# A 31-tap depthwise convolution moves from ScalarE and GpSimd to TensorE, and the steps around it stand in another order

## The reference, cut to what matters

```
def _conformer_conv(v, gt, w_dw, b_dw, ln_g, ln_b, w_pw):
    u = v * jax.nn.sigmoid(gt)
    u = _causal_depthwise_conv(u, w_dw, b_dw)          # 31 taps, 256 channels
    u = jax.nn.silu(_layernorm(u, ln_g, ln_b))
    return u @ w_pw
...
    y_a = _pool_mixer(p_pool, pool_w[l], pool_scale[l])
    y_b = _conformer_conv(p_bval, p_bgate, ...)
    y_c = _rglru_branch(p_cgate, p_cx, ...)            # 4-tap convolution, two gates, scan
    y = jnp.concatenate([y_a, y_b, y_c], axis=-1)
    h = h + y @ w_out[l]
```

## Time and profile before

| | us |
|---|---|
| three runs, median (lowest, highest) | 1353.49 (1351.45, 1354.27) |
| the profiled execution | 1353.51 |
| its span | 1351.7 |
| TensorE busy | 1257.9 (93%) |
| VectorE busy | 875.0 (65%) |
| ScalarE busy | 618.9 (46%) |
| GpSimd busy | 118.4 (9%) |

### The profile page before, as it was taken

One profiled execution on the slowest core, in us unless ns is written; L12 is line 12 of the kernel. 1 busy time (PEld: TensorE's weight loads), 2 busy tenths in 40 slices (PEclk: granted clock), 3 DMA queues, 4 the chain that ended last, 5 costly groups with the idle time before them and its releaser, 6 DMA issues.

```text
span 1351.7 us, 17623 instructions
## 1 busy us (share of the span) xinstructions
PE 1257.9 (93%) x6213; PEld 1026.2 (76%) x6213; DVE 875.0 (65%) x1165; ACT 618.9 (46%) x940; POOL 118.4 (9%) x88
## 2 busy tenths in 40 slices
PE   7899999999988999999998799777999999999997
PEld 5687778777866887777776589775888888888885
DVE  5978888888963456666667667997655522455322
ACT  6456556655652244655565555654332212222112
POOL 0011110111100000000000003581000000000000
PEclk9999999999999999999999799888999999999998
DMA  5333233323323332222221132211323333333332
GB/s 153 110 94 110 78 94 108 94 78 95 107 63 101 93 94 78 74 68 62 65 75 47 40 93 71 63 48 40 97 85 98 99 95 93 93 93 93 109 93 78
DMA packets 203289, 115.57 MB, mean 85 GB/s; under 512 B 3456, under 2 KB 201216, under 8 KB 202224
## 3 DMA queue, kind: packets, MB, share of 16 engines
q1 hardware_dynamic: 201472, 104.50, 26.7%
q0 software_dynamic: 1776, 10.53, 2.3%
HBM read 112.85 MB, written 2.16 MB: 85 GB/s over the span
## 4 chain that ended last, share of the span: by engine, by line
PE 62%; DVE 25%; issue 6%; ACT 6%; DMA 1%; DVEq 0%; SPq 0%; ACTq 0%; POOL 0%
PE psum L510 57%; DVE w_lo L1366 5%; ACT w_hi L922 2%; DVE arena L1801 2%; DVE arena L1439 2%; DVE arena L1657 2%; DVE arena L1440 1%; PE psum L695 1%; DVE arena L1504 1%; DVE mixw L1528 1%; DMA w_raw<-a_w_in 1%; DVE mixw L1532 1%; ACT arena L1119 1%; ACT L1119 1%; DVE arena L1441 1%
## 5 line engine op out<-in xcount | busy, mean ns | idle before, releaser
L922 ACT ACTIVATE w_hi<-w_raw 128x1024 fp32r<-128x1024 f32 x191 | 202.1, 1058 | 503.8 <-PE psum L510 502.0
L510 PE MATMUL psum<-a_hi,w_hi 128*128 128x512 f32 (+1 forms) x1000 | 362.0, 381 | 14.1 <-DVE w_lo L1366 14.1
L510 PE MATMUL psum<-a_lo,w_hi 128*128 128x512 f32 (+1 forms) x1000 | 356.9, 376 | 0.0
L1366 DVE TENSOR_TENSOR w_lo<-w_raw,w_hi 128x1024 fp32r<-128x1024 f32 x191 | 257.4, 1348 | 150.6 <-ACT w_hi L922 150.4
L510 PE MATMUL psum<-a_hi,w_lo 128*128 128x512 f32 (+1 forms) x1000 | 354.7, 373 | 0.0
L510 PE MATMUL psum<-b_hi,w_hi 128*128 128x512 f32 x640 | 256.2, 400 | 8.3 <-DVE b_lo L1545 4.1
L510 PE MATMUL psum<-b_lo,w_hi 128*128 128x512 f32 x640 | 255.2, 399 | 0.0
L510 PE MATMUL psum<-b_hi,w_lo 128*128 128x512 f32 x640 | 253.8, 397 | 0.0
L510 PEld LDWEIGHTS psum<-a_hi,w_hi 128*128 128x128 f32 x1000 | 184.2, 192 | 52.8 <-issue 16.7
L510 PEld LDWEIGHTS psum<-a_hi,w_lo 128*128 128x128 f32 x1000 | 184.3, 192 | 34.0
L510 PEld LDWEIGHTS psum<-a_lo,w_hi 128*128 128x128 f32 x1000 | 184.0, 192 | 31.9
(11 more groups left out here) (269 smaller groups left out, 1317.9 us busy)
## 6 DMA issues: line engine op xcount, KB each, us to landing
w_raw<-a_w_in SPq DMA_DIRECT2D x49, 512.0 KB, 3.9
w_raw<-w_up SPq DMA_DIRECT2D x32, 512.0 KB, 4.0
w_raw<-w_down SPq DMA_DIRECT2D x32, 512.0 KB, 3.7
arena<-acs POOLq DMA_DIRECT2D x8, 1024.0 KB, 5.1
w_raw<-a_w_out SPq DMA_DIRECT2D x16, 512.0 KB, 3.8
w_raw<-w_kv SPq DMA_DIRECT2D x16, 512.0 KB, 3.9
w_raw<-b_w_in SPq DMA_DIRECT2D x16, 512.0 KB, 3.9
w_raw<-w_in SPq DMA_DIRECT2D x14, 512.0 KB, 3.7
```

Source lines behind the costliest of these rows:

```text
L510: ins = mm(out, wv[:, u.par, k, :], xv[:, k0 + k, c0:c0 + cn], start=(first and begin and i == 0 and n == 0), stop=(last and end and i == ...
L922: ac(w_hi[:, u.par, :, :], w_raw[:, u.par, :, :], ACT.Copy).then_inc(S["hi_ready"], 1)
L1366: tt(w_lo[:, u.par, :, :], w_raw[:, u.par, :, :], f32(w_hi[:, u.par, :, :]), ALU.subtract).then_inc(S["lo_ready"], 1)
```

## The change

The second channel tile of the 31-tap convolution is no longer made by ScalarE and GpSimd. The host passes in 31 diagonal matrices with the tap weights (`dwdiag`, padded to 32), eight to a unit, and four more units c0 to c3 stand between the projection's steps. They pass through the same load, high and low halves; TensorE multiplies each diagonal matrix with the tile shifted by the tap, split in high and low parts (`cu_hi`, `cu_lo`), into one bank: 24 products of 512 columns for c0 to c2, 21 for c3. ScalarE then adds the bias in one instruction.

The order is now that of `IN2_STEPS`. The gate sets stand behind steps 5, 6, 8 and 9, in two long and two short pieces with banks of their own. The four projections of the gate branch (steps 10 to 13) leave out the 16 meta tokens and are one product of 512 columns each (`in2_gate`). The first transposes stand behind step 10, the second in front of step 13. On VectorE the layer norm's work moves to step 11, the scans of tiles 2 and 3 stay at step 12 and at the end, the pool means move to steps 10 and 12, and the first tile's taps are spread otherwise. Each step's elementwise work still stands behind that step's high half on ScalarE, and behind its eviction and low half on VectorE. GpSimd waits for the two split copies before the pooling.

```diff
-U_OUT2 = U_IN2 + 14
+U_OUT2 = U_IN2 + 18
+IN2_STEPS = (0, 1, 2, 3, 4, "c0", 5, "c1", 6, "c2", 7, "c3", 8, 9, 10, 11, 12, 13)
...
-            for n, c in enumerate(IN2_TILES):
-                load(Lin(U_IN2 + n), t["w_in_2"], 0, Lin(c * P))
+            for i, n in enumerate(IN2_STEPS):
+                if isinstance(n, str):
+                    load(Lin(U_IN2 + i), t["dwdiag"], KT * int(n[1]), Lin(0))
+                else:
+                    load(Lin(U_IN2 + i), t["w_in_2"], 0, Lin(IN2_TILES[n] * P))
...
-            for k in range(1, DW_K):
-                pool.wait_ge(S["prod_ready"], k + 1)
-                if k > 1:
-                    pool.wait_ge(S["prod_used"], k - 1)
-                nc.gpsimd.tensor_tensor(dwo[:, 1, :], dwo[:, 1, :], products[k % 4][:, 0:SEQ], ALU.add
-                                        ).then_inc(S["prod_used"], 1)
...
+            def in2_gate(n):
+
+                u, m = Lin(U_IN2 + IN2_STEPS.index(n)), Lin(M_IN2 + n)
+                pe.wait_ge(S["acc_read"], (m - 1).v)
+                pe.wait_ge(S["lo_ready"], (u + 1).v)
+                for k in range(KT):
+                    for i, (wv, xv) in enumerate(((w_hi, a_hi), (w_hi, a_lo), (w_lo, a_hi))):
+                        ins = mm(bank(2 * m.par), wv[:, u.par, k, :], xv[:, k, META:T2],
+                                 start=(k == 0 and i == 0), stop=(k == KT - 1 and i == 2), skip_group_check=True)
+                ins.then_inc(S["unit_done"], 1)
+
+            def tap_tile(c):
+
+                u = Lin(U_IN2 + IN2_STEPS.index(f"c{c}"))
+                if c == 0:
+                    pe.wait_ge(S["rr_ready"], 3)
+                    pe.wait_ge(S["cuh_ready"], 1)
+                    pe.wait_ge(S["cul_ready"], 1)
+                pe.wait_ge(S["lo_ready"], (u + 1).v)
+                for j in range(KT):
+                    k = KT * c + j
+                    if k == DW_K:
+                        break
+                    at = DW_K - 1 - k + META
+                    for i, (wv, xv) in enumerate(((w_hi, cu_hi), (w_hi, cu_lo), (w_lo, cu_hi))):
+                        ins = mm(bank(4), wv[:, u.par, j, :], xv[:, at:at + SEQ], start=(k == 0 and i == 0),
+                                 stop=(k == DW_K - 1 and i == 2), skip_group_check=True)
+                ins.then_inc(S["unit_done"], 1)
...
+            in2(4)
+            tap_tile(0)
+            in2(5)
+            gates(0)
+            tap_tile(1)
+            in2(6)
+            gates(1)
+            tap_tile(2)
+            in2(7)
+            tap_tile(3)
+            in2(8)
+            gates(2)
+            in2(9)
+            gates(3)
+            in2_gate(10)
+
+            pe.wait_ge(S["dw_ready"], 1)
+            pe.wait_ge(S["cvo_ready"], 1)
+            pe.wait_ge(S["acc_read"], M_IN2 + 10)
...
+            in2_gate(11)
+            in2_gate(12)
 
             pe.wait_ge(S["ln_ready"], 1)
+            pe.wait_ge(S["rga_ready"], 4)
...
+            in2_gate(13)
...
+                if n == 3:
+                    act.wait_ge(S["cu_ready"], 1)
+                    ac(cu_hi[:, META:], cu[:, 1, META:], ACT.Copy).then_inc(S["cuh_ready"], 1)
+                if n == "c1":
+                    gate_sigmoids(0)
+                if n == "c2":
+                    gate_sigmoids(1)
+                    gate_exps((0, 1))
+                if n == "c3":
+                    gate_roots((0, 1))
                 if n == 8:
-                    gate_roots((0, 1))
...
+                    act.wait_ge(S["unit_done"], U_IN2 + 12)
+                    ac(dwo[:, 1, :], bank(4), ACT.Identity, bias=par[:, C_DWB + 1:C_DWB + 2]).then_inc(S["cvo_ready"], 1)
+                if n == 9:
+                    gate_sigmoids(2)
                 if n == 10:
+                    gate_sigmoids(3)
                     gate_exps((2, 3))
                 if n == 11:
-                    gate_roots((2, 3))
-                if n == 12:
                     act.wait_ge(S["ln_stat"], 1)
                     root(stat_at(N_SD), bnag[:, :, 1], eps2, 1.0, S["ln_sd"])
+                    gate_roots((2, 3))
...
-            TAPS = {1: 3, 2: 5, 3: 3, 4: 2, 5: 2, 6: 1, 7: 1, 8: 3, 9: 5, 10: 5, 11: 1}
+            TAPS = {1: 2, 2: 5, 3: 2, 4: 2, "c0": 4, 5: 2, "c1": 4, 6: 2, "c2": 4, 7: 2, "c3": 2}
...
+                if n == 10:
+                    means(0)
                 if n == 11:
+                    layer_norm_sums()
                     one_minus_a2(2)
                     one_minus_a2(3)
+                    layer_norm()
                 if n == 12:
-                    layer_norm_sums()
                     scan(2)
-                    layer_norm()
-            means(0)
-            means(1)
+                    means(1)
             lo(Lin(U_OUT2 + 1))
             scan(3)
```

More of the change, by code:

```diff
@@ L460, in _ @@
             pool.wait_ge(S["xc_ready"], 4)
+            pool.wait_ge(S["cuh_ready"], 1)
+            pool.wait_ge(S["cul_ready"], 1)
             for j in range(2):
@@ L813, in gates @@
                     pe.wait_ge(S["rga_ready"], j)
[L814 to L818, removed]
+                mm(bank(5), bdw[:, 2 + j, :], xc[:, j, 0:512], start=True, stop=True, skip_group_check=True)
+                mm(bank(6)[:, 0:16], bdw[:, 2 + j, :], xc[:, j, 512:T2], start=True, stop=True, skip_group_check=True)
@@ L820, in _ @@
+                mm(bank(6)[:, 16:512], bdw[:, 6 + j, :], xc[:, j, 0:496], start=True, stop=True, skip_group_check=True)
+                mm(bank(7)[:, 0:32], bdw[:, 6 + j, :], xc[:, j, 496:T2], start=True, stop=True, skip_group_check=True
+                   ).then_inc(S["rg_ready"], 1)
             pe.wait_ge(S["bd_in"], 16)
             pe.wait_ge(S["pw_in"], 16)
[L822 to L834, removed]
-                if n == 12:
[L837 to L844, removed]
@@ new lines, in _ @@
+            in2(1, ks=range(5))
+            pe.wait_ge(S["nrs_ready"], 2)
+            spread(bank(5), stat_at(N_RS), TOKENS1, S["nrb_ready"])
+            tp(bank(7)[:, 0:META], stat[0:META, N_R2 + 4:N_R2 + 5].to_broadcast([META, P]), ident[0:META, 0:META])
+            spread(bank(4), stat_at(N_R2), TOKENS1, S["nrb_ready"])
+            in2(1, ks=range(5, KT))
+            in2(2)
+            in2(3)
+            in2(4)
[3 more added lines that the diff above has]
+            tap_tile(1)
@@ new lines, in _ @@
+            in2(6)
[11 more added lines that the diff above has]
+            pe.wait_ge(S["acc_read"], M_IN2 + 10)
+            for i, (c0, cn) in enumerate(TOKENS1):
+                for j in range(2):
+                    ins = tp(bank(1 + 2 * (i // 2))[:, 256 * (i % 2) + P * j:256 * (i % 2) + P * j + P],
+                             dwo[:, j, c0:c0 + cn], ident)
@@ L1260, in rnn_high @@
                     ac(b_hi[:, 4 + j, 0:SEQ], xc[:, j, META:T2], ACT.Copy).then_inc(S["yh_ready"], 1)
-            PRODUCTS = {3: (0, 5), 4: (5, 9), 5: (9, 13), 6: (13, 17), 7: (17, 20), 8: (20, 24), 9: (24, 28),
-                        10: (28, 31)}
-            for n in range(14):
-                if n:
-                    hi(Lin(U_IN2 + n + 2))
+            for i, n in enumerate(IN2_STEPS):
+                if i:
+                    hi(Lin(U_IN2 + i + 2))
                 if n in (1, 3):
@@ L1857, in layer_norm_sums @@
                 for i in range(NT):
-                    own(nc.vector.bn_stats(bnst[:, i, :], psum[:, 4 + i // 2, 256 * (i % 2):256 * (i % 2) + 256]))
+                    own(nc.vector.bn_stats(bnst[:, i, :], bank(1 + 2 * (i // 2))[:, 256 * (i % 2):256 * (i % 2) + 256]))
                 own.wait()
@@ L2085 @@
         par[:, C_RGW + 4 * j:C_RGW + 4 * j + 4] = x["rg_conv_w_2"][0][:, P * j:P * j + P].T
+    diag = np.zeros((32, P, P), np.float32)
+    for k in range(DW_K):
+        diag[k] = np.diag(x["convb_dw_w_2"][0][DW_K - 1 - k, P:2 * P])
     bd = np.zeros((P, 10, P), np.float32)
```

81 lines of the change are left out of this document (35 added, 46 removed).

## The result

The changed kernel takes 1357.33 us (median of 18 runs, 1353.09 to 1360.47) against 1351.74 us for the kernel before (median of 18, 1348.99 to 1354.63). The ratio is 1.0036, with a 95% interval of 1.0028 to 1.0045: slower by 0.36%, some 5 us. The forecast was 1355.6 with a range of 1349.5 to 1360. The profiled execution took 1357.52 us with a span of 1355.7, against 1353.51 and 1351.7 before: between these two executions the difference is 4.0 us.

The account below looks back on a forecast made before the run. VectorE, slowed by GpSimd's additions, was taken to pace the stage; TensorE's added products, two waits with half clock and a shorter tail summed to 2.1 us over 1353.51: 1355.6 us, range 1349.5 to 1360.

Parts of the forecast that it names:

- VectorE's gain: Second block's input projection: without GpSimd's additions VectorE runs undisturbed, taps 0.78 us; a pair of steps costs 10.8 us.
- Rival 5: Taps slow for another reason than GpSimd, VectorE still pacing the stage: 1374 us; rivals 3 to 5 together 0.07.
- TensorE's added work: Input projection: 31 taps of three products, 21.6 us in all, a unit 5.56 us; gate set taken at 1.94.
- rival 4: Odd columns halve the tap products' rate, adding 21.6 us: 1377 us; rivals 3 to 5 together 0.07.
- First wait: TensorE before the fourth gate set, for the third set's sigmoids: 4.05 us, plus 2.8 us for half clock.
- Rival 1: Clock survives one or both waits, or waits are shorter: 1353 to 1351.3 us, 1350 with cheaper gate sets; chance 0.28.
- Table switches: ScalarE's waiting chains: each switch costed as a 1.28 us load without drain; drains would add 2.8 us.
- rival 3: Every ScalarE table switch costs a drain, adding 2.8 us: 1358.4 us; rivals 3 to 5 together 0.07.
- Second wait: TensorE before the second transposes, for a 15.5 us chain after step 10: 3.6 us, plus 1.55 for half clock.
- The tail: From step 13's end to the output projection: 10.3 us, with 0.3 for GpSimd's multiplication beside the scan, bound 1.8.
- rival 2: GpSimd's multiplication slows the last scan by 1.8 us, first waits' half clock at upper bound: 1357 to 1359; chance 0.18.
- The sum: Output projection starts at 937.5, 2.1 us later than before; everything behind it unchanged: 1355.6 us.

Follow-up runs that it names:

- e5: Kernel before with GpSimd's thirty additions cut to one column each, waits kept, part of the computation left out: 1332.1 us, ratio 0.9860.
- e1: Changed kernel with the fourth gate set behind step 10 instead of in front of it: 1347.61 us, ratio 0.9968.
- e4: Changed kernel with four unread products put into the first wait, to keep the clock: 1354.07 us, ratio 1.0010.
- e11: Changed kernel with GpSimd's third multiplication cut to one column, part of the computation left out: 1354.55 us in one execution.
- e12: The kernel before, unchanged, run once more for a second trace: 1352.13 us in one execution.
- e2: Changed kernel with the layer norm's statistics, root and scalings done earlier, on VectorE and ScalarE: 1355.86 us, ratio 1.0021.
- e3: Changed kernel with both the fourth gate set behind step 10 and the earlier layer norm: 1346.24 us, ratio 0.9958.
- e6: Changed kernel with one tap's products instead of eight in each tap unit, part of the computation left out: 1348.4 us, ratio 0.9979.
- e7: On top of e3, VectorE's second pool means moved behind the last scan: 1350.68 us, ratio 0.9985.
- e8: On top of e4, three more unread products in front of the second transposes: 1352.9 us, ratio 1.0008.
- e9: On top of e3, ScalarE's last two square roots moved behind the next high half: 1348.3 us, ratio 0.9977.
- e10: Changed kernel with the third set's sigmoids ahead of that step's high half on ScalarE: 1356.4 us, ratio 1.0041.

## Why the prediction was right, point by point

**VectorE's gain.** Right. Taps took 0.78 us start to start (3.11 us for four at 841.12 on VectorE's timeline), GpSimd was idle in this stretch until 885, and without its additions the kernel before is 20 us faster (e5). Rival 5 is out.

**TensorE's added work.** Right. A tap unit took 838.55 - 832.96 = 5.59 us where 5.56 was said; odd columns cost nothing, and rival 4 is out. A gate set took 2.06 us start to start where I took 1.94, over the upper bound of 2.0 that I gave. The old form had taken less than I read, since 1.94 is a printed duration; start to start it was 1.59 us, as two rows of the kernel before show:

```profile
876.06 1.94 PE L816 MATMUL psum<-arena,mixw 128*128 128x264 f32 x8
877.65 0.60 PE L510 MATMUL psum<-a_hi,w_hi 128*128 128x264 f32 x2
```

So the new form, two long and two short pieces, costs 0.47 us more for each set with the same columns, and twice that at half clock (4.20 against 3.28). Step 9 ended near 890.3 and not at 889.5: 0.36 from three gate sets, 0.28 from a start that was later in this execution, 0.1 from the tap units.

**First wait.** 3.90 us where 4.05 was said, released by the sigmoids; the 3.90 counts from the modelled end of the last product, and from 890.3, as the forecast counts, it is 4.1. The clock fell as assumed. The set took 4.20 us for 3.28, since I had put the old form's row in its place, and step 10 took 904.74 - 898.58 = 6.16 for 6.99, since less of the half clock was left for it; together 10.4 for 10.3. Moving one line takes wait and clock away together (e1), and unread products take the clock's part alone (e4). Rival 1 is out for this trace.

**Table switches.** From the start of the high half at 890.57 to the load are 1.07 us, to the first sigmoid at 892.94 another 1.30, to the end of the second 1.30, and 0.14 to the gate set at 894.38. The load of 1.28 us follows right on the high half and the sigmoid right on the load, with no room for a drain of 1.38. Here the Trainium skill (ScalarE: Activation LUTs, What ACT_TABLE_LOAD costs) has its load, 1283 ns, borne out and its drain not; rival 3 is out.

**Second wait.** 3.17 for 3.6, on a chain of 920.07 - 904.74 = 15.3 us for 15.5. The transposes took 1.97 us at half clock and step 13 6.33; I had charged the same loss at the other place, 0.82 and 7.1: 8.3 for 7.9. Step 13 ended at 928.4, for 927.2.

**The tail.** 10.9 us for 10.3. This is the term that was mis-sized: I charged 0.3 us for GpSimd's multiplication beside the last scan, with a bound of 1.8. Its first instruction took 1.77 for 0.70, 1.07 more (e11 takes it away). Low half and scan took 934.40 - 929.53 = 4.9 us for 3.8. This is the mechanism of rival 2, at somewhat over half of its bound, and by the 0.7 us of e11 just over the 0.6 us at which the prediction let that rival decide. Its other half, a half clock at its upper bound behind the first waits, did not come.

**The sum.** The output projection started at 939.31, not 937.5: 0.28 from the start, 0.66 before step 10's end, 0.26 by the second wait's chain and clock together, 0.61 in the tail. So the 2.1 us more that were forecast for the stage measured 3.65 in the traces: every mechanism was in place, and the gate sets, the clock behind the second wait and the overlap in the tail were each a little too small in the sum. Behind it nothing changed: it takes 1355.7 - 939.3 = 416.4 us to the end of the span, and 1351.7 - 935.4 = 416.3 before.

**The number.** 1357.33 lies 1.7 us above the forecast of 1355.6, just outside the likeliest case's own range (1353.8 to 1357.2) and inside the wide one (1349.5 to 1360). That it came so near is in part luck. The forecast added 2.1 us to 1353.51, an execution that turned out 1.8 us above the median of the kernel before; the difference itself measured 5.6 us by the medians. The two errors have opposite signs.

**What stays open.** The medians lie 5.6 us apart, the stretches 3.65, and the two profiled executions 4.0. The kernel before has the same stretch in two traces (e12), so the missing 2 us are not the waits of that kernel. Its profiled execution was 1.8 us above its median, the changed kernel's 0.2 above its own: execution against execution almost nothing is missing, and the 2 us appear only between medians of 18. The median less the stretch of the one trace gives what the rest of a kernel takes; all these kernels compute the same, or nearly so, ahead of the stretch and behind it:

| kernel | median us | stretch us | rest us |
|---|---|---|---|
| before | 1351.74 | 102.70 | 1249.0 |
| changed | 1357.33 | 106.35 | 1251.0 |
| e1 gates later | 1347.61 | 98.44 | 1249.2 |
| e2 norm earlier | 1355.86 | 105.50 | 1250.4 |
| e3 both | 1346.24 | 97.70 | 1248.5 |
| e4 keep clock | 1354.07 | 104.96 | 1249.1 |
| e5 no additions | 1332.10 | 83.88 | 1248.2 |
| e6 few products | 1348.40 | 99.46 | 1248.9 |
| e7 scan first | 1350.68 | 100.29 | 1250.4 |
| e8 keep twice | 1352.90 | 102.80 | 1250.1 |
| e9 roots later | 1348.30 | 96.71 | 1251.6 |
| e10 sigmoids first | 1356.40 | 105.80 | 1250.6 |

The rest scatters from 1248.2 to 1251.6, and in the traces the stretch starts between 828.4 and 833.0 us, though the work ahead of it is the same or nearly so. The highest, e9's, holds 1.6 us of half clock behind the stretch. The changed kernel's extra 2 us are of the size of the scatter; what decides it ahead of the stage was not looked into, and whether it is chance or belongs to a kernel's layout is open. It also means that one trace's span is no measure of a change of 0.2%; the stretch between two events is a better one, if its end takes in the clock that the last wait leaves behind.

## What to carry to other kernels

When work is moved to the engine that will then be always busy, walk that engine's queue forward and ask of each wait what the releasing engine has ahead of it. A wait for a chain that only starts when the last unit ends was paid in full here, whatever the sums of busy time said. Put one independent unit between: one line moved turned 0.36% of loss into 0.32% of gain. And price a stall on TensorE with the half clock that may follow it, here 3.9 us of wait and 2.6 of clock. Whether it follows can't be read from the wait's length alone. In the kernel before the granted clock read 0.53 behind a wait of 1.90 us and 1.00 behind one of 2.77:

```profile
848.30:851.70 3.40, 3.40 (x16) 3.40 (x17) 3.33 (x3) 1.99 (x3) 3.11 (x3) 0.53 0.53 154
...
860.40:863.90 3.50, 3.49 (x28) 3.50 (x29) 3.43 (x3) 3.40 (x5) 3.21 (x3) 1.00 0.54 151
```

## What the runs showed of the hardware that was not expected

Products that nobody reads, put into a wait, kept the granted clock up: with 0.47 us of idle time left of 3.9 it read 1.00 from 889.80 to 894.00 (e4), and the gate set's first pair took 0.93 us start to start in place of 1.8. In both moves together, the wait of 4.43 us came behind step 13, and the pooling's products behind it took 3.78 us for 1.99 in the changed kernel, where they followed a wait of 0.78. In e9 it was the output projection that ran at half clock. The price of a stall moved with it to whatever came next.
